# Expert layer of a decoder trunk: h and the gathered tokens are turned in 32x32 blocks by DVE instead of by PE transposes

## What is computed

```python
def swiglu(h, w_gate, w_up, w_down):
    return (jax.nn.silu(h @ w_gate) * (h @ w_up)) @ w_down

def moe(h, w_router, w_gate, w_up, w_down):
    logits = (h @ w_router).astype(jnp.float32)
    top_l, top_i = lax.top_k(logits, TOP_K)
    top_w = jax.nn.softmax(top_l, axis=-1)
    gates = jnp.sum(jax.nn.one_hot(top_i, N_EXPERTS) * top_w[..., None], axis=-2)
    y = jnp.zeros_like(h)
    for e in range(N_EXPERTS):
        y = y + gates[..., e:e + 1] * swiglu(h, w_gate[e], w_up[e], w_down[e])
    return y
```

## Time and profile before

| | |
|---|---|
| median of 3 runs | 1565.88 us (1564.98 to 1567.77) |
| profiled execution | 1568.57 us |
| its span | 1566.8 us |
| PE busy | 1535.2 us (98%) |
| DVE, ACT, POOL busy | 445.6, 366.9, 98.5 us (28%, 23%, 6%) |
| granted TensorE clock, mean | 0.988 |
| DMA read from HBM | 452.26 MB, 289 GB/s over the span |

### The profile page before, as it was taken

One profiled execution on the slowest core, in us unless ns is written; L12 is line 12 of the kernel. 1 busy time (PEld: TensorE's weight loads), 2 busy tenths in 40 slices (PEclk: granted clock), 3 DMA queues, 4 the chain that ended last, 5 costly groups with the idle time before them and its releaser, 6 DMA issues.

```text
span 1566.8 us, 48156 instructions
## 1 busy us (share of the span) xinstructions
PE 1535.2 (98%) x21694; PEld 1130.5 (72%) x21694; DVE 445.6 (28%) x776; ACT 366.9 (23%) x542; POOL 98.5 (6%) x128
## 2 busy tenths in 40 slices
PE   8999999999999999999999999999999999999996
PEld 7999899999899976665666666666666666666664
DVE  6665655455666563001001001001001101101102
ACT  5554444444645431001001001001001001001001
POOL 0550000000253000000000000000000000000000
PEclk9999999999999999999999999999999999999998
DMA  9754445555454546999999999999999999999990
GB/s 322 237 171 153 161 162 188 187 198 180 160 187 165 187 174 228 376 391 346 368 378 362 383 364 371 379 360 382 370 362 382 365 369 378 366 369 378 362 394 35
DMA packets 186547, 456.44 MB, mean 291 GB/s; under 512 B 13760, under 2 KB 79584, under 8 KB 186336
## 3 DMA queue, kind: packets, MB, share of 16 engines
q1 hardware_dynamic: 186336, 453.35, 78.6%
HBM read 452.26 MB, written 1.05 MB: 289 GB/s over the span
## 4 chain that ended last, share of the span: by engine, by line
PE 96%; DVE 1%; ACT 1%; issue 1%; DMA 0%; POOL 0%; SPq 0%; POOLq 0%; DVEq 0%
PE bank L1211 93%; PE bank L1602 2%; DMA gain<-in_ln_dram 0%; PE bank L1628 0%; PE bank L1328 0%; POOL rs L1152 0%; DVE mem L721 0%; ACT mem L494 0%; DVE xt_lo L742 0%; ACT w_hi L471 0%; ACT xt_hi L500 0%; DVE x L750 0%; DVE w_lo L688 0%; PE bank L1244 0%; PE bank L1357 0%
## 5 line engine op out<-in xcount | busy, mean ns | idle before, releaser
L1211 PE MATMUL bank<-mem 128*32 128x256 f32 (+1 forms) x16240 | 891.8, 379 | 1.0 <-issue 0.7
L1211 PEld LDWEIGHTS bank<-mem 128*32 128x32 f32 (+1 forms) x16240 | 525.7, 110 | 345.7 <-issue 7.5
L688 DVE TENSOR_TENSOR w_lo<-mem,w_hi 128x1024 fp32r<-128x1024 f32 x182 | 227.3, 1259 | 176.5 <-ACT w_hi L471 176.0
L1211 PE MATMUL bank<-xt_hi,w_hi 128*128 128x256 f32 x880 | 251.6, 286 | 2.8 <-DVE w_lo L688 2.4
L1211 PE MATMUL bank<-xt_hi,w_lo 128*128 128x256 f32 x880 | 249.9, 284 | 0.0
L1211 PE MATMUL bank<-xt_lo,w_hi 128*128 128x256 f32 x880 | 249.7, 284 | 0.0
L471 ACT CAST w_hi<-mem 128x1024 fp32r<-128x1024 f32 x182 | 189.4, 1049 | 221.6 <-PE bank L1211 217.1
L1211 PEld LDWEIGHTS bank<-xt_hi,w_hi 128*128 128x128 f32 x880 | 167.7, 191 | 5.9 <-issue 4.1
L1211 PEld LDWEIGHTS bank<-xt_lo,w_hi 128*128 128x128 f32 x880 | 167.9, 191 | 0.4
L1211 PEld LDWEIGHTS bank<-xt_hi,w_lo 128*128 128x128 f32 x880 | 167.3, 190 | 0.0
L1114 DVE TENSOR_TENSOR mem<-mem,bank 128x512 f32<-128x512 f32 x24 | 16.5, 688 | 440.4 <-PE bank L1211 440.4
(11 more groups left out here) (179 smaller groups left out, 941.1 us busy)
## 6 DMA issues: line engine op xcount, KB each, us to landing
mem<-in_eg_dram SPq DMA_DIRECT2D x224, 512.0 KB, 6.5
mem<-in_eu_dram SPq DMA_DIRECT2D x224, 512.0 KB, 6.7
mem<-in_ed_dram SPq DMA_DIRECT2D x224, 512.0 KB, 6.9
mem<-in_w_in_dram SPq DMA_DIRECT2D x42, 1024.0 KB, 5.3
mem<-in_fg_dram SPq DMA_DIRECT2D x11, 1024.0 KB, 5.2
mem<-in_fu_dram SPq DMA_DIRECT2D x11, 1024.0 KB, 5.2
mem<-in_fd_dram SPq DMA_DIRECT2D x11, 1024.0 KB, 4.8
mem<-in_w_br_dram SPq DMA_DIRECT2D x8, 1024.0 KB, 4.9
```

Source lines behind the costliest of these rows:

```text
L688: nc.vector.tensor_tensor(w_lo[:, q % H, :], src, w_hi[:, q % H, :].bitcast(F32), ALU.subtract).then_inc(lo_done, 1)
L1211: return nc.tensor.matmul(out, lhs, rhs, start=first, stop=last, skip_group_check=True)
```

## The change

Gate and up units, and the gather, use another assignment of channels to column tiles: tile q takes every fourth run of 32 columns (128j + 32q + r) and not 256 adjacent ones. Then a plain 32x32 block transpose of DVE, which works within 32 partitions, puts channel 128j + 32q + r on partition 32q + r, as the down matmuls want it. The six PE transposes per step, ACT's copies of them and the copies of raw sums go. The gather now has perm's 32 columns as weights and hn as the moving operand, in column tiles, and DVE turns its banks into ex. It moves behind all eight halves of the third step's down unit. ACT's silu waits until DVE has read the silu of the step before. The scatters are rearranged for items beyond the eighth only.

```diff
-        ex = carve(W_HALVES * HALF, KT, SLOTS)
+        ex = carve(W_HALVES * HALF, GROUPS, KT, 32)
...
+        def mixed(n, h):
+
+            return bank[n][:, :].rearrange("p (g h n) -> p g h n", g=2, h=2)[:, :, h, :]
...
-                def hidden_copy(s):
-
-                    act.wait_ge(t_full, ESTEPS * i + s + 1)
-                    nc.scalar.copy(eh[s % 2][:, 0:512], bank[6][:, :])
-                    nc.scalar.copy(eh[s % 2][:, 512:768], bank[7][:, 0:256]).then_inc(eh_done, 1)
+                    act.wait_ge(half_used, ITEM_HALVES * i + G_AT[s] + 8 + 1)
+                    if s:
+                        act.wait_ge(ehf_done, 2 * ESTEPS * i + 2 * s)
...
+            def gather_turn(item):
+
+                flat = ex.rearrange("p g k s -> p (g k s)")
+                dve.wait_ge(gather_full, 2 * item + 1)
+                nc.vector.transpose(flat[:, 0:512], bank[0][:, :])
+                dve.wait_ge(gather_full, 2 * item + 2)
+                nc.vector.transpose(flat[:, 512:768], bank[1][:, 0:256]).then_inc(ex_done, 1)
...
+                    dve.wait_ge(esg_done, silu + 1)
+                    if s < LAST:
+                        h = mhf
+                        nc.vector.tensor_tensor(h[:, 0:two], msg[:, 0:two], bank[2][:, :], ALU.mult).then_inc(ehf_done, 1)
+                    else:
+                        h = msg
+                        h2 = h[:, 0:two].rearrange("p (g n) -> p g n", g=2)
+                        nc.vector.tensor_tensor(h2, h2, mixed(0, 1), ALU.mult).then_inc(ehf_done, 1)
+                    dve.wait_ge(esg_done, silu + 2)
+                    up = bank[3][:, 0:256] if s < LAST else mixed(1, 1)[:, 0, :]
+                    nc.vector.tensor_tensor(h[:, two:two + one], msg[:, two:two + one], up, ALU.mult).then_inc(ehf_done, 1)
+                    dve.wait_ge(ehf_done, silu + 1)
+                    nc.vector.transpose(eh[s % 2][:, 0:two], h[:, 0:two])
+                    dve.wait_ge(ehf_done, silu + 2)
+                    nc.vector.transpose(eh[s % 2][:, two:two + one], h[:, two:two + one]).then_inc(eh_done, 1)
...
+            def strided(w, q):
+
+                return w.rearrange("p (j q r) -> p j q r", q=4, r=32)[:, :, q, :]
+
+            def gather():
+
+                for g in range(GROUPS):
+                    cols = slice(g % 2 * 256, (g % 2 + 1) * 256)
                     for t in range(TB):
-                        ins = mm(bank[m][:, d * SLOTS:(d + 1) * SLOTS], hn[:, t, dd * P:(dd + 1) * P],
-                                 perm[:, t, :, 0:32].bitcast(F32), d == 0 and t == 0, d == 3 and t == TB - 1)
-                ins.then_inc(gather_full, 1)
+                        for q in range(4):
+                            ins = mm(bank[g // 2][32 * q:32 * q + 32, cols], perm[:, t, g, 0:32].bitcast(F32),
+                                     strided(hn[:, t, :], q), t == 0 and g % 2 == 0, t == TB - 1)
+                    if g:
+                        ins.then_inc(gather_full, 1)
...
-                            ins = mm(banks[g // 2][32 * q:32 * q + 32, cols], ex[:, kk, 32 * g:32 * g + 32],
-                                     w[:, q * 256:(q + 1) * 256], kk == 0 and g % 2 == 0, kk == KT - 1)
+                            ins = mm(banks[g // 2][32 * q:32 * q + 32, cols], ex[:, g, kk, :],
+                                     strided(w, q), kk == 0 and g % 2 == 0, kk == KT - 1)
...
-            def transposes(src):
-
-                for k in range(6):
-                    ins = nc.tensor.transpose(bank[6 + k // 4][:, k % 4 * P:(k % 4 + 1) * P], src[:, k * P:(k + 1) * P], ident)
-                ins.then_inc(t_full, 1)
...
+                for s in range(1, LAST):
+                    pe.wait_ge(esg_done, 2 * ESTEPS * i + 2 * s)
+                    wide_unit(i, gate_banks, G_AT[s], range(8))
+                    pe.wait_ge(ehf_done, 2 * ESTEPS * i + 2 * s)
+                    wide_unit(i, up_banks, U_AT[s], range(8))
+                    pe.wait_ge(eh_done, ESTEPS * i + s)
+                    expert_down(i, s - 1, range(8))
+                pe.wait_ge(esg_done, 2 * ESTEPS * i + 2 * LAST)
+                wide_unit(i, gate_banks, G_AT[LAST], range(8))
+                pe.wait_ge(eh_done, ESTEPS * i + LAST)
+                expert_down(i, LAST - 1, range(8))
                 if more:
                     gather_next(i)
...
-                pe.wait_ge(eh_last, i + 1)
+                pe.wait_ge(eh_done, ESTEPS * i + ESTEPS)
                 expert_down(i, LAST, range(4))
+                pe.wait_ge(pt_done, i + 1)
```

More of the change, by code:

```diff
@@ L657, in _ @@
                 nc.scalar.copy(perm_t[:, 512:768], bank[7][:, 0:256]).then_inc(pt_done, 1)
-                hidden_copy(0)
-                for s in range(1, LAST):
+                for s in range(1, ESTEPS):
                     gate_silu(s)
[L661 to L668, removed]
             output_split(ITEM_HALVES * n_items + 1)
@@ L1110, in hidden @@
                 def hidden(s):
[L1112 to L1116, removed]
+                    used, silu = (U_AT[s] if s < LAST else G_AT[s]) + 8, 2 * ESTEPS * i + 2 * s
+                    dve.wait_ge(half_used, ITEM_HALVES * i + used + 1)
+                    two, one = WIDTH[s] // 2, WIDTH[s] // 4
+                    dve.wait_ge(esg_done, silu + 1)
+                    if s < LAST:
+                        h = mhf
+                        nc.vector.tensor_tensor(h[:, 0:two], msg[:, 0:two], bank[2][:, :], ALU.mult).then_inc(ehf_done, 1)
+                    else:
+                        h = msg
[8 more added lines that the diff above has]
+                    nc.vector.transpose(eh[s % 2][:, two:two + one], h[:, two:two + one]).then_inc(eh_done, 1)
+                    if s < LAST:
+                        dve.wait_ge(eh_done, ESTEPS * i + s + 1)
                 output_split(2 * i)
@@ L1123, in _ @@
                 make_perm(bass.ds(i + 1, 1))
-                for s in range(1, LAST):
+                for s in range(1, ESTEPS):
                     hidden(s)
-                dve.wait_ge(half_used, ITEM_HALVES * i + D_AT[LAST - 1] + 1)
-                nc.vector.tensor_copy(msg[:, 512:768], bank[1][:, 0:256]).then_inc(mix_v, 1)
                 with dve.If(n_items > i + 1):
[L1129 to L1134, removed]
+                    gather_turn(i + 1)
             output_split(2 * n_items)
@@ L1563, in _ @@
             pe.wait_ge(perm_done, 1)
-            for m in range(2):
-                gather(m)
+            gather()
             def half(i, n):
@@ L1597, in expert_down, with item @@
                     ins.then_inc(half_used, 1)
-            def transposes(src):
-                for k in range(6):
-                    ins = nc.tensor.transpose(bank[6 + k // 4][:, k % 4 * P:(k % 4 + 1) * P], src[:, k * P:(k + 1) * P], ident)
-                ins.then_inc(t_full, 1)
             def gather_next(i):
                 pe.wait_ge(perm_done, i + 2)
[L1608 to L1611, removed]
+                pe.wait_ge(ehf_done, 2 * ESTEPS * (i + 1))
+                gather()
             gate_banks, up_banks = (bank[0], bank[1]), (bank[2], bank[3])
-            def item(i, more):
-                pe.wait_ge(ex_a, i + 1)
-                pe.wait_ge(ex_v, i + 1)
+            def item(i, more, lead):
+                pe.wait_ge(ex_done, i + 1)
                 wide_unit(i, gate_banks, G_AT[0], range(8))
-                scatter(0, i + 1)
+                if lead:
+                    scatter(0, i + 1)
                 wide_unit(i, up_banks, U_AT[0], range(4))
-                pe.wait_ge(scat_done, 4 * i + 2)
-                scatter(1, i + 1)
+                if lead:
+                    pe.wait_ge(scat_done, 4 * i + 2)
+                    scatter(1, i + 1)
                 wide_unit(i, up_banks, U_AT[0], range(4, 8))
@@ L1646, in item, with scatter_last @@
                         gather_next(i)
[L1647 to L1651, removed]
-                pe.wait_ge(eh_last, i + 1)
-                expert_down(i, LAST, range(4))
+                pe.wait_ge(eh_done, ESTEPS * i + ESTEPS)
+                expert_down(i, LAST, range(4))
+                pe.wait_ge(pt_done, i + 1)
+            def scatter_last(count):
+                scatter(0, count + 1)
+                pe.wait_ge(scat_done, 4 * count + 2)
+                scatter(1, count + 1)
             for i in range(NE - 1):
-                item(i, True)
+                item(i, True, True)
             pe.wait_ge(routed, 1)
             n_items = pe.value_load(items[0:1, 0:1], min_val=NE, max_val=MAX_ITEMS)
-            item(NE - 1, False)
+            item(NE - 1, False, True)
+            scatter_last(NE)
             with pe.If(n_items > NE):
                 with pe.Fori(NE, n_items) as i:
[L1662 to L1665, removed]
+                    item(i, False, False)
+                    scatter_last(i + 1)
 def kernel(**inputs):
```

36 lines of the change are left out of this document (10 added, 26 removed).

## The result

The changed kernel takes 1523.47 us (median of 4 runs, 1522.69 to 1523.72) against 1565.43 (4 runs, 1564.58 to 1567.77): ratio 0.9729, 95% interval 0.9712 to 0.9746.

The account below looks back on a forecast made before the run. The prediction took PE to bound the kernel. Removed transposes 25.9, the gather 8.0 and first gather 1.8 summed to 35.7 us, so 1565.88 - 35.7 = 1530.2 us, range 1525 to 1545.

Parts of the forecast that it names:

- Bound: Expert stage: PE sets the pace, busy 119.47 of 119.47 us a period, with the loads as second candidate.
- Removed transposes: Four groups of six PE transposes an item, 0.81 us each, seams included, over 8 items: 25.9 us gained.
- The gather: Between items: 48 instructions in 2.60 us instead of 32 in 3.75, no seam; 1.15 us, 7 times: 8.0 us.
- First gather: Gather ahead of the first item, at clock 0.50: 5.2 us instead of 6.87, gain taken as 1.8 us.
- The last scatters: End of the expert stage: scatters said to be in the same places for 8 items, so no gain counted.
- Strides: Gate, up and gather columns in eight runs of 32: taken as free; rival of costing more than the gain, 0.10.
- turns: DVE transposes replacing PE's, 0.69 and 0.42 us, all hidden behind PE's work; rival of a late turn, 0.01.
- loads: Weight loads in the items: 382.6 GB/s needed, PE still bound; rival of loads binding in part 0.08, wholly 0.02.

Follow-up runs that it names:

- e2: Changed kernel with six 128x128 PE transposes, read by nobody, put back at four places of each item: 1553.51 us.
- e3: Changed kernel with eight matmuls of the weight stream's own shape, read by nobody, at four places of each item: 1550.81 us.
- e5: Changed kernel with the gather in its old form (32 instructions, 128 weight columns of hn) in its new place: 1534.96 us.
- e1: Changed kernel with 256 adjacent moving columns per column tile again, in gate and up units and the gather: 1524.42 us.
- e8: Changed kernel with 11 more matmuls on zeros in PE's waits before the first gather: 1523.75 us.
- e12: Kernel before the change with only the last two scatters moved ahead of the branch: 1565.33 us beside 1567.04, ratio 0.9979.
- e4: Changed kernel with the last two scatters back behind the branch and the loop for items beyond the eighth: 1524.35 us.
- e7: Changed kernel with every DVE turn of h done twice and the last turn of the gathered tokens three times: 1524.13 us.
- e6: Changed kernel with the third token group's products left out of the expert units, all loads kept: 1474.75 us.
- e10: The kernel before the change, unedited, profiled once more: 1567.03 us.
- e11: The changed kernel, unedited, run once more: 1523.35 us.

## Why the prediction was too cautious, step by step

**Bound.** Right. PE had 96% of the chain before and after, and no wait on a load appeared in the items. (The slices of the earlier trace rows reach 394 GB/s, not 391; nothing hangs on that.)

**Removed transposes.** The mechanism was right, the term was mis-sized. The step that failed is "each 0.81 us on the chain, seams included, since the chain's steps are contiguous". The steps are contiguous, but the cost of coming back to 32-column tiles stands in the row of the matmuls behind, as e2 and e3 show. A group is 0.945 us: 32 x 0.945 = 30.2 us and not 25.9. The same slip made a half 1.301 us where it is 1.295.

**The gather.** Its seam was missing for the same reason. 1.28 us each, as e5 shows, and not 1.15: 9.0 us for seven, not 8.0. With four groups and a gather the period falls by 3.78 + 1.28 = 5.06 us, which is what the two chains show (119.47 to 114.40). This step is the bulk of the miss, 5.3 us.

**First gather.** The forecast had 5.2 us at the clock's lower level; it took 4.10, since the clock came back inside it. The range of the term (-1.4 to 4.4) held it; the gain was 2.9 against 1.8. Its upper end could not be reached: with the clock up, PE waits for DVE, which is at the routing until 594, and goes on 4.1 us after the gather's start (e1, e8), a gain of 3.5. The clock in the earlier trace rows falls at 590.2, not 590.6: the row's 0.61 is a mean. Nothing hangs on that.

**The last scatters.** Costed at nothing: "The scatters are in the same places for 8 items". They are, in order, but not in the program: the last two moved from behind a branch to ahead of it, so the rearrangement wasn't for items beyond the eighth only. The tail became 2.2 us shorter, some 1.5 of waiting and 0.7 of clock. e12 shows that the move alone brings this to the kernel before; e4 shows that the rest of the change brings all but 0.2 us of it without the move. Neither had a term in the sum, and how the 2.2 us divide between them has no single answer.

**Strides, turns, loads.** Free, as forecast (e1, e7). The rate was forecast at about 385 GB/s and is 386. The Trainium skill's bound of some 358 GB/s for a core (DMA: Bandwidth & Descriptors, Where 436 GB/s comes from) does not hold here: e6 had 402 GB/s over 800 us. The Trainium skill's rule of 16-byte lines (SBUF — State Buffer, Door 1: The DMA port swizzle), by which runs of whole lines are no dearer than adjacent columns, agrees with e1 (113.61 us both ways).

**The sum again.** 30.2 + 9.0 + 2.9 + 2.2 = 44.3 us. The medians of the kernel before lie between 1565.4 and 1568.8 us, so the change is worth 42 to 45 us; where both kernels ran in one set again, it was 1567.51 - 1523.35 = 44.2. The range's lower end, 1525, came from an upside of a few us in the first gather and none in the largest term, whose price I had held for exact.

## What to carry to other kernels

Price an interruption of a stream by the period with and without it, or from two stretches of different length, each behind one, and not by the interrupting instructions' own row: the seam hides in the stretch behind. In a kernel whose stream runs in 32-column tiles, a 128x128 instruction among them costs more than its time, and work that can be put in the stream's own shape, or on an idle engine, has no seam. Read each line of a diff that moves code across a branch as a possible change of time. And before hunting for more on PE, ask the loads: here some 4 us an item are left until they are the bound.

## What the runs showed of the hardware

- 32-column tiles and back: 0.14 us for each return from six 128x128 transposes (e2), 0.13 from matmuls with 128 weight columns (e5), none for other work in the same shape (e3).
- Moving operands in runs of 32 columns, 512 bytes apart, four tiles at once, are as fast as adjacent ones (e1).
- Loads of 512 KB reach 402 GB/s sustained on this core, at a DMA share of 1.02; a share of 0.98 came with 371 (e6).
- Behind a branch PE went on 1.6 us after what it waited for in one program (e10) and 0.33 in another (e4), against 0.14 and 0.04 with the work ahead of the branch (changed kernel, e12).
- The clock's behaviour at the first gather varies between profiles: at 0.50 for 3.4 us in the changed kernel and in e11, at 1.00 throughout in e1, e3 and e7, none of which has fillers, and in e8, which has. With the old gather it stood at 0.50 for 6.8 us (before, e5).
